# Attention's inverse sums as a diagonal factor in the transposes, in a two-layer sparse-attention and mixture trunk

## The chip, the cores and the metric

One NeuronCore of a Trainium2 chip runs the whole program. The metric is the device time of one execution in microseconds (us). The engines are TensorE (PE; its weight loads are PEld in the profile), VectorE (DVE), ScalarE (ACT), GpSimd (POOL) and SyncE (SP, which issues the weight DMAs). Each takes its own instructions in order; semaphores tie them together.

## The reference

Two layers, each of a mixer and a mixture of experts over 512 tokens of width 1024. The change concerns the attention of the mixer only. Its core, cut:

```python
score = einsum(relu(q_idx . k_idx), w_idx)            # indexer, 8 heads
_, sel = lax.top_k(where(admissible, score, -inf), 128)
logits = einsum('bqhd,bqkhd->bqhk', qb, k_sel) * att_scale   # 8 heads of 64
p = softmax(where(sel_ok, logits, -inf), axis=-1)
y_a = einsum('bqhk,bqkhd->bqhd', p, v_sel)            # queries in 4 blocks of 128
...
x = x + concat([y_a, y_pool, y_conv]) @ w_out
x = x + hier_moe(rmsnorm(x))                          # 16 experts, 6 MB of weights each
```

The softmax divides by the sum of the exponentials. The kernel does not gather: it adds a mask to the full row of logits, so that keys not chosen come out as zero.

## The kernel before, in words

Each layer projects the input (products of float32 split into a high and a low half, three products each), runs the indexer and 16 rounds of top-k on VectorE while TensorE makes the later projections, then the attention stage, the output projection, routing, and 16 experts whose weights stream through a ring of slots.

The attention stage is 16 **units**: query block b = unit // 4 (128 queries, 128·(b+1) keys) and head pair j = unit % 4, with d = 0, 1 the two heads of the pair. The order is written out by hand as a software pipeline over **steps** s:

- TensorE in step s: the logits of unit s (`unit_qk`, L1015), the transposes of unit s−2 (`unit_turn`, L1039, one `T.transpose` of 128x128 for each head and key block), the product with V of unit s−3 (`unit_pv`, L1029), in steps 7, 11, 15 and 17 the spreading of inverse sums (`spread_rinv`, L1049), in steps 10 and 11 the convolution branch's products (L1089), in 12 and 13 the pooling branch's (L1099). Units 0 to 2's logits and unit 0's transposes are interleaved with the projection of V. Before the logits of steps 4, 5 and 6 stand 4, 2 and 2 products of constants (`spin`, L693) that nobody reads.
- VectorE in step s: mask and row minimum of unit s (L1983, two instructions; its output is the buffer `probs[s % 2]`, so it waits until unit s−2 has been transposed), then `other(s)`: low halves of output weights in steps 4, 7, 10 and 15 (`lo`, L436), the branches' low halves in steps 11 to 14 (L1961, L1966), in steps 5, 9, 13 reciprocals of 8 sums (`o_inverse`, L1943), in 8, 12, 16 `o_scale` (L1951 copies the spread inverses out of bank 2, L1952 multiplies PV's bank with them into `osb`), and one step later `o_lo` (L1935). After `other`, in steps 3 to 9, one part of the pooling branch (L1619 to L1636).
- ScalarE: exponentials of unit s with their sums into `stat` (`unit_exp`, L1377), copies of the transposed unit s−2 to SBUF (`unit_pt`, L1385), and in its own `other` the high halves (L431, L1365, L1393, L1398).

The logits of both heads have one bank each, so `unit_qk(s)` waits until VectorE has read both of unit s−1. After the last step TensorE goes straight on to the output projection. A matmul whose operands are float32 is two records in the trace; a transpose, and a product of the split halves, is one.

Of the kernel before, what the change touches and what calls it, by code (L numbers as in the profile page):

```python
# [111 lines left out]
SPREAD_UNIT, SCALE_UNIT, HALF_UNIT = (7, 11, 15, 17), (8, 12, 16), (9, 13, 17)  # L112
# [39 lines left out]
def trunk(nc, t, out):  # L152
    with ExitStack() as ctx:
# [72 lines left out]
        osb = ar(A_O, 512)  # L226
# [38 lines left out]
        for name, dims in (("lg", (TT, 20)), ("gd", (TT, 4)), ("ge", (TT, 4)), ("og", (TT, 4)), ("key", (E - FIXED,)), ("place", (E,)), ("perm", (E,)),   # L265
# [49 lines left out]
        qk_ready, logit_set, exp_set, pt_ready, pt_set, pv_ready, rinv_set, r_ready, o_set = (  # L315
            sem(n) for n in ("qk_ready", "logit_set", "exp_set", "pt_ready", "pt_set", "pv_ready", "rinv_set", "r_ready", "o_set"))
# [370 lines left out]
        def _(pe):  # L687
# [290 lines left out]
            for l in range(DEPTH):  # L978
# [39 lines left out]
                def unit_pv(w):  # L1018

                    b, j = w // PAIRS, w % PAIRS  # L1020
                    if w == 0:
                        pe.wait_ge(v_set, 4 * (l + 1))
                    pe.wait_ge(pt_set, HEAD_UNITS * l + 2 * w + 2)
                    if j == 0 and b >= 2:
                        pe.wait_ge(o_set, TT * l + b - 1)
                    for kb in range(b + 1):
                        for d in range(2):
                            h = 2 * j + d
                            mm = T.matmul(ps[d * 64:d * 64 + 64, b % 2, j * P:(j + 1) * P], v_sb[:, kb, h * HD:(h + 1) * HD],  # L1029
                                          pTs[w % 2][:, d, kb * P:(kb + 1) * P], start=(kb == 0), stop=(kb == b))  # L1030
                    mm.then_inc(pv_ready, 1)

                def unit_turn(w):
                    for d in range(2):
                        pe.wait_ge(exp_set, HEAD_UNITS * l + 2 * w + d + 1)
                        if w:
                            pe.wait_ge(pt_set, HEAD_UNITS * l + 2 * w - 1 + d)
                        for kb in range(w // PAIRS + 1):
                            mm = T.transpose(ps[:, 6 + d, kb * P:(kb + 1) * P], probs[w % 2][:, d, kb * P:(kb + 1) * P], ident)  # L1039
                        mm.then_inc(pt_ready, 1)  # L1040

                def spread_rinv(b):

                    pe.wait_ge(rinv_set, TT * l + b + 1)
                    if b:
                        pe.wait_ge(o_set, TT * l + b)
                    for j in range(PAIRS):
                        for d in range(2):
                            mm = T.matmul(ps[d * 64:d * 64 + 64, 2, j * P:(j + 1) * P],  # L1049
                                          rinv[:, 2 * j + d:2 * j + d + 1].to_broadcast([P, HD]), ident, start=True, stop=True)  # L1050
                    mm.then_inc(r_ready, 1)
# [64 lines left out]
                for s in range(len(QK_AT), UNITS + 3):  # L1116
# [8 lines left out]
                    if s in SPREAD_UNIT:  # L1125
                        spread_rinv(SPREAD_UNIT.index(s))
# [10 lines left out]
                for i in range(4):  # L1137
                    use(pe, n + i)
                    for tt in ((2, 3, 1, 0) if i == 0 else range(TT)):
                        if i == 0 and tt == 1:  # L1140
                            pe.wait_ge(o_set, TT * (l + 1))
                        for h in range(2):
                            mm = out_product(i, tt, h)
                    mm.then_inc(w_used, 1)
# [45 lines left out]
        def _(sc):  # L1190
# [103 lines left out]
            for l in range(DEPTH):  # L1294
# [68 lines left out]
                def o_hi(b):  # L1363
                    sc.wait_ge(o_set, TT * l + b + 1)
                    A.activation(a_hi[:, 0:4, b * P:(b + 1) * P], osb.rearrange("p (q n) -> p q n", q=4),  # L1365
# [96 lines left out]
        def _(ve):  # L1462
# [402 lines left out]
            for l in range(DEPTH):  # L1865
# [67 lines left out]
                def o_lo(b):  # L1933
                    ve.wait_ge(o_hi_set, TT * l + b + 1)
                    V.tensor_tensor(a_lo[:, 0:4, b * P:(b + 1) * P], osb.rearrange("p (q n) -> p q n", q=4),  # L1935
                                    a_hi[:, 0:4, b * P:(b + 1) * P].bitcast(F32), ALU.subtract).then_inc(o_lo_set, 1)

                def o_inverse(b):

                    ve.wait_ge(exp_set, HEAD_UNITS * l + HEADS * (b + 1))  # L1940
                    if b:
                        ve.wait_ge(r_ready, TT * l + b)
                    V.reciprocal(rinv[:], stat[:, 1, HEADS * b:HEADS * (b + 1)]).then_inc(rinv_set, 1)  # L1943

                def o_scale(b):

                    ve.wait_ge(r_ready, TT * l + b + 1)
                    ve.wait_ge(pv_ready, UNITS * l + PAIRS * (b + 1))
                    if b:
                        ve.wait_ge(o_lo_set, TT * l + b)  # L1950
                    link(V.tensor_copy(osb, ps[:, 2, :]))  # L1951
                    V.tensor_tensor(osb, ps[:, b % 2, :], osb, ALU.mult).then_inc(o_set, 1)  # L1952

                def other(s):
# [13 lines left out]
                    if s in (5, 9, 13):  # L1968
                        o_inverse((s - 5) // PAIRS)
                    if s - 1 in HALF_UNIT:  # L1970
                        o_lo(HALF_UNIT.index(s - 1))
                    if s in SCALE_UNIT:
                        o_scale(SCALE_UNIT.index(s))

                def unit(s):
# [9 lines left out]
                    other(s)  # L1985
                    if 3 <= s < 10:
                        pooling(l, s - 3)
# [33 lines left out]
                for s in range(4, UNITS):  # L2021
                    unit(s)
                other(UNITS)
                o_inverse(TT - 1)
                other(UNITS + 1)
                other(UNITS + 2)
                o_scale(TT - 1)
# [112 lines left out]
```

## Time and profile before

| | |
|---|---|
| median of 3 runs | 1111.81 us (1110.94 to 1113.27) |
| the profiled execution | 1111.22 us, of which the profile's span is 1108.9 us |
| TensorE busy | 1043.9 us (94%) |
| VectorE, ScalarE busy | 548.9 us (49%), 292.3 us (26%) |
| granted TensorE clock, mean | 0.984 |

The span is cut by what TensorE does: projections and indexer from 0 to 151 us, attention (steps 3 to 18, from the logits of unit 3 to the output projection) from 165.7 to 221.0 us, output projection and routing to 285 us, experts to 520 us, then the second layer with the same stages 545.94 us later. A time in a row is counted from the start of the span. A row's duration holds its latency, and records of one engine overlap: how fast instructions follow each other is read from the distance of starts.

### The profile page before, as it was taken

What the parts mean: (1) busy time and instruction counts of PE and PEld (TensorE: products, weight loads), DVE (VectorE), ACT (ScalarE), POOL (GpSimd) and SP (SyncE); (2) the same over time, 40 slices, a digit from 0 to 9 for tenths busy, and PEclk for the clock granted to TensorE, in tenths of its full rate; (3) what the DMA queues carried; (4) which work ended last, traced back from release to release, by engine and by line L of the source; (5) the groups of instructions that cost most, each with busy time, mean ns of one, the idle gap of its engine ahead of it and who ended that gap; (6) DMA issues with size and microseconds to landing.
All of it is one profiled execution on the core that took longest, in us unless ns stands there. A gap on an engine that the chain in (4) does not pass through costs nothing.

```text
span 1108.9 us, 26835 instructions
## 1 busy us (share of the span) xinstructions
PE 1043.9 (94%) x11416; PEld 769.3 (69%) x11416; DVE 548.9 (49%) x1260; ACT 292.3 (26%) x570; POOL 192.0 (17%) x265
## 2 busy tenths in 40 slices
PE   8999998999999999997889999989999999999875
PEld 7876874587778777763478677646877988677432
DVE  5999987525611111110679999764364012101108
ACT  5225346623000010010252343465230000000003
POOL 3300000000323332231300000000003332233220
PEclk9999999999999999998999999999999999999988
DMA  9742211054989999999944122012479799999994
GB/s 358 235 193 77 84 50 57 21 209 179 405 319 341 401 401 403 406 403 406 351 147 133 57 89 92 24 45 70 177 289 396 269 394 404 402 402 404 407 399 188
DMA packets 86903, 279.63 MB, mean 252 GB/s; under 512 B 12344, under 2 KB 12448, under 8 KB 86768
## 3 DMA queue, kind: packets, MB, share of 16 engines
q1 hardware_dynamic: 71040, 237.60, 56.3%
q0 software_dynamic: 15728, 40.15, 10.0%
q8 instruction: 94, 1.54, 0.6%
q14 instruction: 41, 0.34, 0.1%
HBM read 257.43 MB, written 23.07 MB: 253 GB/s over the span
## 4 chain that ended last, share of the span: by engine, by line
PE 69%; DVE 15%; DMA 6%; issue 3%; ACT 3%; SPq 3%; POOL 1%; POOLq 0%; DVEq 0%; ACTq 0%
PE ps L852 24%; PE ps L892 11%; DVE arena L1611 7%; PE ps L455 7%; PE ps L457 7%; PE ps L456 7%; DMA arena<-in_w_dn 3%; SPq L406 3%; DVE w_lo L436 2%; PE ps L1039 2%; PE ps L1015 1%; PE ps L1029 1%; PE ps L998 1%; DMA arena<-y_rows,yidx 1%; PE ps L693 1%
## 5 line engine op out<-in xcount | busy, mean ns | idle before, releaser
L1827 DVE SCALAR_TENSOR_TENSOR arena<-ps,gslot,arena 128x128 f32<-128x128 f32 x88 | 25.7, 345 | 385.6 <-ACT arena L1250 368.4
L852 PE MATMUL ps<-arena 128*32 128x256 f32 x2624 | 155.3, 380 | 3.8 <-DMA arena<-in_w_gu 2.8
L852 PE MATMUL ps<-raw,arena 128*32 128x256 f32 x2528 | 149.9, 380 | 6.9 <-DMA raw<-in_w_gu 6.2
L852 PEld LDWEIGHTS ps<-arena 128*32 128x32 f32 x2624 | 113.0, 110 | 41.6 <-issue 8.0
L852 PEld LDWEIGHTS ps<-raw,arena 128*32 128x32 f32 x2528 | 102.8, 110 | 48.7 <-DMA raw<-in_w_gu 12.4
L631 POOL DMA_INDIRECT gain<-h_rows,tab x82 | 85.0, 1036 | 249.1 <-DVE arena L1819 206.1
L455 PE MATMUL ps<-a_hi,w_hi 128*128 128x512 f32 (+1 forms) x304 | 121.7, 400 | 3.1 <-DVE w_lo L436 2.1
L457 PE MATMUL ps<-a_hi,w_lo 128*128 128x512 f32 (+1 forms) x304 | 118.7, 390 | 0.0
L456 PE MATMUL ps<-a_lo,w_hi 128*128 128x512 f32 (+1 forms) x304 | 118.6, 390 | 0.0
L431 ACT ACTIVATE w_hi<-raw 128x1024 fp32r<-128x1024 f32 (+1 forms) x64 | 65.0, 1022 | 131.9 <-PE ps L457 130.7
L1250 ACT ACTIVATE arena<-ps 128x384 f32<-128x384 f32 (+1 forms) x32 | 14.9, 465 | 308.8 <-PE ps L852 266.9
L436 DVE TENSOR_TENSOR w_lo<-raw,w_hi 128x1024 fp32r<-128x1024 f32 (+1 forms) x64 | 74.8, 1172 | 34.5 <-ACT w_hi L431 34.3
L1611 DVE SCALAR_TENSOR_TENSOR arena<-arena,chan 128x512 f32<-128x512 f32 x120 | 84.2, 747 | 1.3
L640 POOL DMA_DIRECT2D y_rows<-arena x112 | 63.2, 575 | 101.9 <-ACT arena L1258 97.6
L892 PE MATMUL ps<-arena,pw 128*32 128x256 f32 x1088 | 68.3, 399 | 8.4 <-DMA arena<-in_w_dn 8.4
L455 PE MATMUL ps<-w_hi,a_hi 128*128 128x512 f32 x192 | 76.2, 397 | 0.0
L457 PE MATMUL ps<-w_hi,a_lo 128*128 128x512 f32 x192 | 74.9, 390 | 0.0
L456 PE MATMUL ps<-w_lo,a_hi 128*128 128x512 f32 x192 | 74.8, 390 | 0.0
L455 PEld LDWEIGHTS ps<-a_hi,w_hi 128*128 128x128 f32 (+1 forms) x304 | 56.3, 185 | 22.6 <-issue 7.7
L892 PE MATMUL ps<-raw,arena 128*32 128x256 f32 x1184 | 71.0, 379 | 0.6 <-DMA raw<-in_w_dn 0.6
L577 POOL DMA_DIRECT2D gain<-in_norm_g x2 | 1.1, 540 | 398.5 <-PE ps L1029 398.5
L457 PEld LDWEIGHTS ps<-a_hi,w_lo 128*128 128x128 f32 (+1 forms) x304 | 56.3, 185 | 13.2
(260 smaller groups left out, 1437.8 us busy)
## 6 DMA issues: line engine op xcount, KB each, us to landing
arena<-in_w_gu SPq DMA_DIRECT2D x120, 512.0 KB
raw<-in_w_gu SPq DMA_DIRECT2D x116, 512.0 KB
raw<-in_w_dn SPq DMA_DIRECT2D x68, 512.0 KB
arena<-in_w_dn SPq DMA_DIRECT2D x48, 512.0 KB
raw<-in_w_in SPq DMA_DIRECT2D x40, 512.0 KB
deep<-in_w_gu SPq DMA_DIRECT2D x20, 512.0 KB, 7.6
y_rows<-arena POOLq DMA_DIRECT2D x96, 96.0 KB
raw<-in_w_out SPq DMA_DIRECT2D x16, 512.0 KB
```

The costliest lines, as they stand in the source:

```text
L406: sp.dma_start(at_slot(slot_of[n], w), src.rearrange("p (a n) -> p a n", a=2)).then_inc(landed(n)[0], 16)
L431: nc.scalar.activation(split_slot(w_hi, k, w), at_slot(slot_of[n], w), ACT.Copy).then_inc(w_hi_set, 1)
L436: nc.vector.tensor_tensor(split_slot(w_lo, k, w), at_slot(slot_of[n], w), split_slot(w_hi, k, w).bitcast(F32), ALU.subtract).then_inc(w_lo ...
L455: nc.tensor.matmul(o, lh, rh, start=start, stop=False)
L456: nc.tensor.matmul(o, lh, rl, start=False, stop=False)
L457: return nc.tensor.matmul(o, ll, rh, start=False, stop=stop)
L631: pool.indirect_dma_start(xg[:, s * QC:(s + 1) * QC], None, h2q[l], bass.IndirectOffsetOnAxis(ap=tab[:, s, e:e + 1], axis=0), bounds_check ...
L640: pool.dma_start(rows[c], ysb[G * c:G * c + G, 0:GROUPS_OF[e] * QC].rearrange("i (s n) -> i s n", n=QC)).then_inc(y_stored, 16)
L852: mm = T.matmul(o, rows, piece[:, :, c * P:(c + 1) * P], start=b == 0, stop=b == 7)
L892: mm = T.matmul(ps[G * c:G * c + G, D_BANK + s, 0:QC], act, piece[:, c // 2, c % 2 * QC:(c % 2 + 1) * QC], start=b == 0, stop=b == 3)
L1611: V.scalar_tensor_tensor(out=acc[:, m, :], in0=src, scalar=w, in1=acc[:, m, :], op0=ALU.mult, op1=ALU.add).then_inc(conv_tap, 1)
L1827: ins = V.scalar_tensor_tensor(out=slu[:, s, :], in0=hidden(e, 1)[:, s, :], scalar=gslot[:, s, e:e + 1], in1=slu[:, s, :], op0=ALU.mult, o ...
```

## The change

`spread_rinv`, `o_inverse`, `o_scale` and the buffer `osb` go. For each unit, VectorE now takes the reciprocals of its two sums and multiplies the identity with each, which makes two 128x128 diagonals in the place of `osb` (two units deep). The transpose of the probabilities becomes an ordinary float32 product of the probabilities with that diagonal, which transposes and scales at once. The high and low halves of the output are then taken directly from PV's bank, and the waits on `o_set` become waits on `o_lo_set`, `pv_ready` and `diag_set`.

```diff
-SPREAD_UNIT, SCALE_UNIT, HALF_UNIT = (7, 11, 15, 17), (8, 12, 16), (9, 13, 17)
+HALF_UNIT = (7, 11, 15)
...
-        osb = ar(A_O, 512)
+        diags = ar(A_O, 512).rearrange("p (u d n) -> p u d n", u=2, d=2)
...
                     if j == 0 and b >= 2:
-                        pe.wait_ge(o_set, TT * l + b - 1)
+                        pe.wait_ge(o_lo_set, TT * l + b - 1)
...
                 def unit_turn(w):
                     for d in range(2):
-                        pe.wait_ge(exp_set, HEAD_UNITS * l + 2 * w + d + 1)
+                        pe.wait_ge(diag_set, UNITS * l + w + 1)
                         if w:
                             pe.wait_ge(pt_set, HEAD_UNITS * l + 2 * w - 1 + d)
                         for kb in range(w // PAIRS + 1):
-                            mm = T.transpose(ps[:, 6 + d, kb * P:(kb + 1) * P], probs[w % 2][:, d, kb * P:(kb + 1) * P], ident)
+                            mm = T.matmul(ps[:, 6 + d, kb * P:(kb + 1) * P], probs[w % 2][:, d, kb * P:(kb + 1) * P], diags[:, w % 2, d, :],
+                                          start=True, stop=True)
                         mm.then_inc(pt_ready, 1)
-                def spread_rinv(b):
...
-                    if s in SPREAD_UNIT:
-                        spread_rinv(SPREAD_UNIT.index(s))
...
-                        if i == 0 and tt == 1:
-                            pe.wait_ge(o_set, TT * (l + 1))
+                        if i == 0 and tt == 0:
+                            pe.wait_ge(o_lo_set, TT * (l + 1))
...
                 def o_hi(b):
-                    sc.wait_ge(o_set, TT * l + b + 1)
-                    A.activation(a_hi[:, 0:4, b * P:(b + 1) * P], osb.rearrange("p (q n) -> p q n", q=4),
+                    sc.wait_ge(pv_ready, UNITS * l + PAIRS * (b + 1))
+                    A.activation(a_hi[:, 0:4, b * P:(b + 1) * P], ps[:, b % 2, :].rearrange("p (q n) -> p q n", q=4),
                                  ACT.Copy).then_inc(o_hi_set, 1)
...
-                def o_inverse(b):
...
-                def o_scale(b):
...
+                def unit_diag(w):
+
+                    q = 2 * w
+                    inverse = rinv[:, q % HEADS:q % HEADS + 2]
+                    ve.wait_ge(exp_set, HEAD_UNITS * l + q + 2)
+                    V.reciprocal(inverse, stat[:, 1, q:q + 2]).then_inc(rinv_set, 1)
+                    ve.wait_ge(rinv_set, UNITS * l + w + 1)
+                    V.tensor_tensor(diags[:, w % 2], ident.unsqueeze(1).to_broadcast([P, 2, P]), inverse.unsqueeze(2).to_broadcast([P, 2, P]),
+                                    ALU.mult).then_inc(diag_set, 1)
...
                     other(s)
+                    if s:
+                        unit_diag(s - 1)
                     if 3 <= s < 10:
                         pooling(l, s - 3)
...
+                unit_diag(UNITS - 1)
                 other(UNITS)
-                o_inverse(TT - 1)
                 other(UNITS + 1)
                 other(UNITS + 2)
-                o_scale(TT - 1)
                 o_lo(TT - 1)
```

In VectorE's order, steps 7 and 8 of the first layer before (the last mask instruction of step 7 on; L436 is the low half, L1632 the pooling branch, L1951 and L1952 `o_scale`):

```order
L1983 ISA arena,stat<-ps,arena 128x256
L1983 ISA stat 128x1
L436 TENSOR_TENSOR w_lo<-raw,w_hi 128x1024
L1632 SCALAR_TENSOR_TENSOR arena<-arena,cst 64x512 x2
L1983 ISA arena,stat<-ps,arena 128x384
L1983 ISA stat 128x1
L1983 ISA arena,stat<-ps,arena 128x384
L1983 ISA stat 128x1
L1951 COPY arena<-ps 128x512
L1952 TENSOR_TENSOR arena<-ps,arena 128x512
L1632 SCALAR_TENSOR_TENSOR arena<-arena,cst 64x512 x2
```

The same place now (in the changed file L1961 is the mask instruction, L1931 and L1933 the diagonals, L1620 the pooling branch, L1923 `o_lo`):

```order
L436 TENSOR_TENSOR w_lo<-raw,w_hi 128x1024
L1931 RECIPROCAL rinv<-stat 128x2
L1933 TENSOR_TENSOR arena<-cst,rinv 128x256
L1620 SCALAR_TENSOR_TENSOR arena<-arena,cst 64x512 x2
L1961 ISA arena,stat<-ps,arena 128x384
L1961 ISA stat 128x1
L1961 ISA arena,stat<-ps,arena 128x384
L1961 ISA stat 128x1
L1923 TENSOR_TENSOR a_lo<-ps,a_hi 128x4x128
L1931 RECIPROCAL rinv<-stat 128x2
L1933 TENSOR_TENSOR arena<-cst,rinv 128x256
L1620 SCALAR_TENSOR_TENSOR arena<-arena,cst 64x512 x2
```

Copy and multiply have gone from step 8, where the low half of the output now stands, and a reciprocal and a product with the identity stand in every step, behind `other` and ahead of the pooling branch.

VectorE's last steps of the first layer before (step 15 on):

```order
L1983 ISA arena,stat<-ps,arena 128x512
L1983 ISA stat 128x1
L436 TENSOR_TENSOR w_lo<-raw,w_hi 128x1024
L1951 COPY arena<-ps 128x512
L1952 TENSOR_TENSOR arena<-ps,arena 128x512
L1943 RECIPROCAL rinv<-stat 128x8
L1935 TENSOR_TENSOR a_lo<-arena,a_hi 128x4x128
L1951 COPY arena<-ps 128x512
L1952 TENSOR_TENSOR arena<-ps,arena 128x512
L1935 TENSOR_TENSOR a_lo<-arena,a_hi 128x4x128
L436 TENSOR_TENSOR w_lo<-raw,w_hi 128x1024 x4
```

And now (from the second head's mask of step 15):

```order
L1961 ISA arena,stat<-ps,arena 128x512
L1961 ISA stat 128x1
L436 TENSOR_TENSOR w_lo<-raw,w_hi 128x1024
L1931 RECIPROCAL rinv<-stat 128x2
L1933 TENSOR_TENSOR arena<-cst,rinv 128x256
L1931 RECIPROCAL rinv<-stat 128x2
L1933 TENSOR_TENSOR arena<-cst,rinv 128x256
L1923 TENSOR_TENSOR a_lo<-ps,a_hi 128x4x128 x2
L436 TENSOR_TENSOR w_lo<-raw,w_hi 128x1024 x4
```

The diagonals of units 14 and 15 stand behind the low half of step 15 (L436).

TensorE from step 15 to the end of the stage, before (L1015 logits, L1039 transposes, L1029 product with V, L1049 the spreading):

```order
L1015 MATMUL ps<-arena 128x512 x2
L1039 MATMUL ps<-cst,arena 128x128 x8
L1029 MATMUL ps<-arena 64x128 x8
L1049 MATMUL ps<-cst,rinv 64x128 x8
L1039 MATMUL ps<-cst,arena 128x128 x8
L1029 MATMUL ps<-gain,arena 64x128 x8
L1039 MATMUL ps<-cst,arena 128x128 x8
L1029 MATMUL ps<-arena 64x128 x8
L1049 MATMUL ps<-cst,rinv 64x128 x8
L1029 MATMUL ps<-gain,arena 64x128 x8
```

And now (L1039 is the product with the diagonal):

```order
L1015 MATMUL ps<-arena 128x512 x2
L1039 MATMUL ps<-arena 128x128 x8
L1029 MATMUL ps<-arena 64x128 x8
L1039 MATMUL ps<-arena 128x128 x8
L1029 MATMUL ps<-gain,arena 64x128 x8
L1039 MATMUL ps<-arena 128x128 x8
L1029 MATMUL ps<-arena 64x128 x8
```

Each spreading row is gone and each transpose has become a float32 product.

## Rows read from the trace of the kernel before

**Rows 1.** The page's fourth part: chain that ended last, share by engine.

```profile
PE 69%; DVE 15%; DMA 6%; issue 3%; ACT 3%; SPq 3%; POOL 1%; POOLq 0%; DVEq 0%; ACTq 0%
```

**Rows 2.** Groups of TensorE instructions by form: xcount, busy us, mean ns, idle before.

```profile
L1039 PE MATMUL ps<-cst,arena 128*128 128x128 f32 x160 | 28.3, 296 | 4.7 <-ACT arena L1385 4.3
L1049 PE MATMUL ps<-cst,rinv 128*64 128x128 f32 x128 | 8.3, 273 | 0.0
L714 PE MATMUL ps<-arena,x_sb 128*128 128x128 f32 x32 | 3.9, 275 | 0.0
```

**Rows 3.** Timeline of TensorE, 8.8 to 15 us: start, duration, instructions.

```profile
10.28 2.78 PE L713 MATMUL ps<-cst,arena 128*128 128x128 f32 x24
12.90 1.95 PE L714 MATMUL ps<-arena,x_sb 128*128 128x128 f32 x16
```

**Rows 4.** Timeline of TensorE in the first layer's attention.

```profile
171.34 0.70 PE L1015 MATMUL ps<-arena 64*128 64x256 f32 x4
...
174.39 0.70 PE L1015 MATMUL ps<-arena 64*128 64x256 f32 x4 [0.59 <-DVE stat L1983]
...
179.84 0.92 PE L1015 MATMUL ps<-arena 64*128 64x384 f32 x4
...
186.54 1.28 PE L1015 MATMUL ps<-arena 64*128 64x384 f32 x4 [1.35 <-DVE stat L1983]
187.75 1.54 PE L1039 MATMUL ps<-cst,arena 128*128 128x128 f32 x6
...
192.22 0.92 PE L1015 MATMUL ps<-arena 64*128 64x384 f32 x4
193.07 0.87 PE L1039 MATMUL ps<-cst,arena 128*128 128x128 f32 x6
...
194.58 1.04 PE L1049 MATMUL ps<-cst,rinv 128*64 128x128 f32 x16
195.55 1.98 PE L1089 MATMUL ps<-arena,pw 128*128 128x512 f32 x4
197.47 1.13 PE L1015 MATMUL ps<-arena 64*128 64x512 f32 x4
...
202.30 1.13 PE L1015 MATMUL ps<-arena 64*128 64x512 f32 x4
...
207.14 1.13 PE L1015 MATMUL ps<-arena 64*128 64x512 f32 x4
208.20 1.09 PE L1039 MATMUL ps<-cst,arena 128*128 128x128 f32 x8
...
210.37 1.13 PE L1015 MATMUL ps<-arena 64*128 64x512 f32 x4 [0.27 <-DVE stat L1983]
...
214.81 1.40 PE L1039 MATMUL ps<-cst,arena 128*128 128x128 f32 x8
...
220.96 0.50 PE L455 MATMUL ps<-w_hi,a_hi 128*128 128x512 f32 x1
```

**Rows 5.** Timeline of VectorE in the same stretch.

```profile
178.95 1.22 DVE L436 TENSOR_TENSOR w_lo<-raw,w_hi 128x1024 fp32r<-128x1024 f32 x1
180.08 1.50 DVE L1632 SCALAR_TENSOR_TENSOR arena<-arena,cst 64x512 f32<-64x512 f32 x2
...
182.58 0.69 DVE L1951 COPY arena<-ps 128x512 f32<-128x512 f32 x1
183.30 0.69 DVE L1952 TENSOR_TENSOR arena<-ps,arena 128x512 f32<-128x512 f32 x1
...
205.95 0.19 DVE L1943 RECIPROCAL rinv<-stat 128x8 f32<-128x8 f32 x1
```

**Rows 6.** Line L1902, a product with a broadcast operand.

```profile
L1902 DVE TENSOR_TENSOR rw<-rw,gcol x1: 476/476/476, 44.0 to 44.0; 128x320 f32<-128x320 f32 x1
```

**Rows 7.** Windows: width, busy of PE, PEld, DVE, ACT, POOL; clock; DMA share; GB/s.

```profile
187.00:190.00 3.00, 3.00 (x18) 1.86 (x14) 1.12 (x5) 2.00 (x7) 0.00 (x0) 0.50 0.00 0
...
310.00:330.00 20.00, 20.00 (x373) 16.83 (x366) 4.85 (x14) 1.78 (x3) 6.37 (x8) 1.00 0.87 329
```

## What the change will do to the time, and why

> **What bounds the kernel now.** I read the chain of waits first [rows 1]: TensorE holds 69% of it, VectorE 15%, DMA 6%. So a microsecond of TensorE work counts unless it falls into a gap. Next come the forms of the instructions that change [rows 2], then how fast such instructions follow each other [rows 3], because durations of overlapping records say little. The timelines of the attention stage [rows 4, 5] show a pipeline that is nearly closed. TensorE's time between starts of a step's logits is 5.25 us in step 11 (192.22 to 197.47), 4.83 us in step 12 (to 202.30), 3.23 us in step 14 (207.14 to 210.37), and only gaps of 0.3 to 1.4 us stand in it, all until VectorE has masked the logits. One more thing is to be seen: in step 10 (186.54 to 192.22, 5.68 us) the logits take 1.28 us where step 11's take 0.92 us, since the granted clock from 187 to 190 us was 0.50, the 1.2 GHz level, after TensorE had sat idle for 1.35 us [rows 4, 7].
>
> **The products.** `T.transpose` is one record: 160 in two layers, 80 a layer [rows 2]. A float32 product is two. L714 is such a product with a diagonal, as the new ones are, and shows its pace: L713's 24 transposes start at 10.28 and L714 at 12.90 us, 2.62/24 = 0.109 us each; L714's 16 records, for 8 products, take 1.95 us with a tail of some 0.16 us, 0.112 us each [rows 3]. So a product costs two times a transpose, and 80 more records a layer are 80 x 0.11 = 8.8 us. The spreading goes: 64 records a layer, 0.97 us for the 16 of each block (194.58 to 195.55) [rows 2, 4], 3.9 us a layer. Net TensorE work +4.9 us a layer.
> The Trainium skill speaks against this edit: "Perfetto Trace Analysis", Transposes, asks that logical transposes use the transpose and not a standard matmul. Its page "TensorE: Matmul & The Clock Gate" (Terms) puts the transpose mode at 4 times the speed for float32; by that a product would add 0.33 us instead of 0.11 us, an estimate of 26 us a layer. The records of rows 3 say two times, and I take them.
>
> **The diagonals.** VectorE gets, for each of 16 units, a reciprocal of 128x2 and a product of 128x256. The reciprocal of 128x8 takes 0.19 us [rows 5]. A product with a broadcast operand of 128x320 takes 0.476 us [rows 6], so 128x256 takes some 0.42 us; the wait between the two costs little, as L1952 starts 0.72 us after L1951, whose duration is 0.69 us [rows 5]. Since starts follow closer than durations, I take 0.57 us a unit; bounds are 0.45 (full overlap) and 0.9 us (if broadcasting both operands were twice as slow). That is 9 us of VectorE a layer, against 4 x (0.19 + 1.4) = 6.4 us removed. It costs time only where TensorE waits for it: `unit_diag(s-1)` is behind the masks and `other` of step s, and TensorE's products of step s+1 need it. They stand behind the logits of step s+1, which give 0.42 to 1.06 us of cover. A low half (1.13 us, 178.95 to 180.08 [rows 5]) in `other` breaks that cover; it stands in steps 4, 7, 10, 15. Taking the halves from PV's bank costs nothing new: `o_hi` and `o_lo` leave a chain with the copy and multiply ahead of them, and the last `o_lo` must be done only after 18 products of the output projection, some 4 us. With it done some 1.5 us after the last PV, nothing waits.
>
> **Step by step, each layer**, with starts of the first layer [rows 4] (the second repeats them):
> - Up to step 10's start (186.54): the small turns of units 0 to 2 add 2 records each, 0.22 us, of which some 0.55 us in sum reaches step 5 (171.34). Diagonal 3 comes behind the low half of step 4, so TensorE, which had other waits of 0.3 us there, waits till some 2 us after step 5's start and step 6 starts 0.9 us late (174.39 before). Step 7's larger turn makes that 1.1 us; then the spreading goes and step 8 (179.84) is 0.3 us late. Diagonal 6 is behind the low half of step 7 and then the pooling branch's 1.50 us delays the masks; the 1.4 us of copy and multiply of step 8 go, 0.7 us of `o_lo` and 0.57 us of diagonal come. Step 10 starts 1.5 us late. **+1.5**
> - Step 10: logits 0.85, turn 0.80 + 0.65 for 6 more records, PV 0.5, the convolution product 1.92 us, 4.75 us in sum at full clock, where 5.68 us were. I take the low clock to go (below). **-0.9**
> - Step 11: no spreading, but L1089 must wait until VectorE has written the low half of the product before it, behind masks that follow the larger turn: 5.7 against 5.25 us. **+0.45**
> - Steps 12, 13: the pooling product waits in the same way; the second mask starts after both turns instead of back to back with the first, 0.43 us later each. **+0.85**
> - Step 14: turn 1.05 -> 1.88 us (8 more records), and the next logits wait for the second mask: 3.23 -> 3.97 us. **+0.75**
> - Step 15 to the turn of unit 14 (210.37 to 214.81, 4.44 us): TensorE would need 1.2 + 1.88 + 1.0 = 4.1 us, but diagonal 14 stands behind two masks that end 4.0 us after the step's start, the low half (1.13 us) and its own 0.57 us: 5.8 us, of which TensorE idles 1.7 us. **+1.35**
> - From there to the output projection (214.81 to 220.96): two turns with 8 more records each, +1.75 us, less the spreading (0.9) and a wait of 0.3 us. **+0.55**
>
> Sum 4.55 us a layer, 9.1 us in two. Behind the stage nothing takes it back: from 310 to 330 us the DMA share was 0.87, so the weights waited for slots there, and slots are freed by expert products that start after attention [rows 7]. The profiled execution's 1111.22 us + 9.1 = 1120.3 us; its own time is 0.6 us under the median of 1111.81, so the forecast is 1120.9, said as 1121 us, slower by 0.8%.
>
> **The rivals.**
> - *The low clock stays.* What speaks for it: TensorE still idles between steps 8 and 10 (some 3 us of 8). Against it: its busy share there is no smaller, with twice the records in the turns. Price: step 10 is then 1.5 us longer in each layer, +3.0 us: 1124 us. The page on the clock gate (PE-mode transpose) says that a transpose does not count as busy as a product does; by that the change itself would lift the clock. The trace shows only that the clock fell where transposes, gaps and small products mixed [rows 4, 7]; that bears on my choice a little.
> - *The diagonals come in time.* If ScalarE's and VectorE's orders slide so that waits at steps 5, 8 and 9 are hidden in waits that exist anyway, some 1.7 us a layer goes: 1117.5 us.
> - *Faster.* The masking and exponentials, not TensorE, set the period, and a second record runs in time that TensorE spends waiting. Then only the losses by diagonals stay: +0.9 up to step 10, -1.5 in step 10 (clock and nothing added), 0 in 11 to 14, +0.45 in step 15, -1.2 after it with the spreading gone: -1.35 us a layer, 1109 us. It decides if the gaps in steps 11 to 15 exceed 0.11 us x the added records (0.65 to 0.9 us). Rows 4 show gaps of 0.3 us in step 14 and 15, and none before the turns: against it.
> - *Slower still.* The idle 1.7 us ahead of unit 14's turn brings the clock down for the last turns, PV and the first output products (as after 186.54, 1.6 us for one fall), on top of the low clock at step 10: 1111.8 + 9.1 + 3.0 + 3.2 = 1127 us.
> - *Absorbed.* The experts end on weight transfers, and a longer attention lets the ring fill further: within 0.2%. Against it: the share of 0.87 above, and that the slots depend on attention's own end.
>
> **How the numbers follow.** Chances: forecast 0.47, low clock stays 0.20, diagonals in time 0.12, slower still 0.08, absorbed 0.06, faster 0.07. The range from 1114 to 1127 us takes in the first four and the ends of the cost of a diagonal (0.12 us less or 0.33 us more at some 5 places in each layer, -1.2 or +3.3 us). Within 0.2% (2.2 us, about what a measurement tells from no change) is 0.07, faster 0.07, slower 0.86.
>
> **What would show it.** In the new profile: two records for each product of the turns, at a pace of 0.11 us, 320 in all; none of L1049; the reciprocal and product of a unit in some 0.57 us; the granted clock near step 10; a gap of some 1.7 us ahead of unit 14's turn with VectorE's diagonal as its releaser; the stage (from the logits of unit 3 to the output projection) 59.8 us long where it was 55.2 us. The forecast is wrong if that stage grows by under 2 us, or if the experts start late and end in time.

## The result, and the profile after

The changed kernel takes 1124.55 us (median of 4 runs, 1123.56 to 1125.22) where the kernel before, measured with it, takes 1111.38 us (4 runs, 1108.71 to 1113.27). The ratio is 1.012, 95% interval 1.0097 to 1.0142: slower by 13.2 us, where the forecast was 9.1 us more and 1121 us. The profiled execution took 1123.56 us, span 1121.3 us, 12.4 us over the span before.

First the page of the kernel after: its busy row and the shares of the chain that ended last.

```profile
PE 1053.0 (94%) x11448; PEld 789.6 (70%) x11448; DVE 553.6 (49%) x1300; ACT 292.5 (26%) x570; POOL 192.0 (17%) x265
...
PE 68%; DVE 16%; DMA 6%; SPq 5%; issue 3%; ACT 2%; POOL 1%; DVEq 0%; POOLq 0%; ACTq 0%
```

TensorE is busy 9.1 us longer (1043.9 before), VectorE 4.7 us, and nothing has changed in who bounds the kernel [rows 1]. The groups by form show the edit itself (busy us, mean ns, idle before):

```profile
L1039 PE MATMUL ps<-arena 128*128 128x128 f32 x320 | 44.8, 286 | 8.8 <-DVE arena L1933 6.7 <-ACT arena L1373 1.8
...
L1933 DVE TENSOR_TENSOR arena<-cst,rinv 128x256 f32<-128x256 f32 x32 | 13.6, 425 | 1.1
```

L1039 has 320 records where it had 160, L1049 is gone [rows 2], and what ended most of TensorE's idle time before L1039 is now VectorE's diagonal (6.7 us), where it was ScalarE's copy (4.3 us). Busy time alone does not tell the price: the timeline does. Of TensorE in the first layer's attention, with step 3 at the top and the output projection's first product at the end:

```profile
165.61 0.49 PE L1015 MATMUL ps<-arena 64*128 64x128 f32 x4
...
171.67 0.70 PE L1015 MATMUL ps<-arena 64*128 64x256 f32 x4
...
173.19 0.71 PE L1039 MATMUL ps<-arena 128*128 128x128 f32 x4 [0.81 <-DVE arena L1933]
...
181.87 1.16 PE L1039 MATMUL ps<-arena 128*128 128x128 f32 x8 [0.76 <-DVE arena L1933]
...
188.00 0.92 PE L1015 MATMUL ps<-arena 64*128 64x384 f32 x4 [0.75 <-DVE stat L1961]
188.85 1.60 PE L1039 MATMUL ps<-arena 128*128 128x128 f32 x12
...
192.88 0.92 PE L1015 MATMUL ps<-arena 64*128 64x384 f32 x4
...
196.76 1.98 PE L1079 MATMUL ps<-arena,pw 128*128 128x512 f32 x4 [0.62 <-DVE a_lo L1943]
198.68 1.13 PE L1015 MATMUL ps<-arena 64*128 64x512 f32 x4
...
202.91 1.12 PE L1089 MATMUL ps<-arena,pbd 128*128 128x512 f32 x2 [0.76 <-DVE a_lo L1943]
...
209.25 1.13 PE L1015 MATMUL ps<-arena 64*128 64x512 f32 x4
210.30 2.05 PE L1039 MATMUL ps<-arena 128*128 128x128 f32 x16
212.29 0.88 PE L1029 MATMUL ps<-gain,arena 128*64 128x128 f32 x12
213.26 1.13 PE L1015 MATMUL ps<-arena 64*128 64x512 f32 x4
...
219.08 2.05 PE L1039 MATMUL ps<-arena 128*128 128x128 f32 x16 [1.55 <-DVE arena L1933]
...
225.96 0.50 PE L455 MATMUL ps<-w_hi,a_hi 128*128 128x512 f32 x1
```

Set against [rows 4], the stage from 165.61 to 225.96 takes 60.35 us, where it took 55.24 us (165.72 to 220.96). The second layer has 60.36 and 55.24 us. A turn with eight transposes (1.09 us) is a turn with 16 records (2.05 us). The 1.55 us wait stands where the prediction put it. VectorE in front of it:

```profile
216.65 0.69 DVE L1961 CUSTOM_DVE_ANT_0 arena<-ps,arena 128x512 f32<-128x512 f32 x1 [0.19 <-PE ps L1039]
...
217.27 1.22 DVE L436 TENSOR_TENSOR w_lo<-raw,w_hi 128x1024 fp32r<-128x1024 f32 x1
218.40 0.16 DVE L1931 RECIPROCAL rinv<-stat 128x2 f32<-128x2 f32 x1
218.60 0.43 DVE L1933 TENSOR_TENSOR arena<-cst,rinv 128x256 f32<-128x256 f32 x1
218.94 0.16 DVE L1931 RECIPROCAL rinv<-stat 128x2 f32<-128x2 f32 x1
```

The mask of step 15, the low half of an output weight, then the diagonal of unit 14, which is what TensorE waits for from 217.53 to 219.08 us. From reciprocal to reciprocal a diagonal takes 0.54 us. The clock in two windows (width, busy of the five engines, clock, DMA share, GB/s):

```profile
187.00:190.00 3.00, 2.25 (x20) 1.46 (x16) 1.62 (x8) 1.83 (x6) 0.00 (x0) 1.00 0.00 0
...
217.00:220.00 3.00, 1.45 (x18) 1.21 (x15) 2.93 (x8) 2.46 (x7) 0.00 (x0) 1.00 0.15 16
```

The first window had 0.50 before [rows 7]; now TensorE keeps 2.4 GHz there, and across the 1.55 us wait too.

Outside the attention stages a difference of 2.2 us is left. One microsecond of it lies between the layers. TensorE's products of constants there, after and then before:

```profile
557.47 0.79 PE L693 MATMUL ps<-cst 128*128 128x128 f32 x2 [3.76 <-DVE x_sb L1548]
...
561.45 0.79 PE L693 MATMUL ps<-cst 128*128 128x128 f32 x2 [3.19 <-issue]
```

```profile
552.02 3.67 PE L693 MATMUL ps<-cst 128*128 128x128 f32 x16 [3.67 <-DVE x_sb L1560]
```

"issue" is idle time that ended on nothing the profile shows: TensorE stood for 3.19 us in the middle of its products of constants. Before, the 16 products ran without a break. From the landing of the gathered rows of layer 1 to the first projection product of layer 2 (L455) it takes 16.39 us where it took 15.35. The rest is 0.4 us in the first layer's experts (271.5 against 271.1 us from their first product, L832, to that landing) and 0.6 us from the second layer's first expert product to the end (286.27 against 285.69).

### The profile page after: what moved, and what is told of

Its sections match the earlier page's. It is cut to its first block, busy times and chain, and to the rows that moved or that the text cites. A ratio compares the mean times of both kernels' runs of the same rounds, so it can differ in the third digit from the quotient of the medians.

```text
span 1121.3 us, 26919 instructions
## 1 busy us (share of the span) xinstructions
PE 1053.0 (94%) x11448; PEld 789.6 (70%) x11448; DVE 553.6 (49%) x1300; ACT 292.5 (26%) x570; POOL 192.0 (17%) x265
## 4 chain that ended last, share of the span: by engine, by line
PE 68%; DVE 16%; DMA 6%; SPq 5%; issue 3%; ACT 2%; POOL 1%; DVEq 0%; POOLq 0%; ACTq 0%
PE ps L852 23%; PE ps L892 10%; DVE arena L1599 7%; PE ps L455 7%; PE ps L457 7%; PE ps L456 7%; SPq L406 4%; DMA arena<-in_w_gu 3%; PE ps L1039 3%; DVE w_lo L436 2%; DVE arena L1961 1%; DMA arena<-in_w_dn 1%; PE ps L1015 1%; PE ps L693 1%; PE ps L897 1%
## 5 line engine op out<-in xcount | busy, mean ns | idle before, releaser
L852 PEld LDWEIGHTS ps<-arena 128*32 128x32 f32 x2624 | 115.4, 110 | 38.9 <-issue 8.4
L455 PE MATMUL ps<-a_hi,w_hi 128*128 128x512 f32 (+1 forms) x304 | 121.7, 400 | 2.8 <-DVE w_lo L436 2.1
L436 DVE TENSOR_TENSOR w_lo<-raw,w_hi 128x1024 fp32r<-128x1024 f32 (+1 forms) x64 | 74.7, 1169 | 37.6 <-ACT w_hi L431 37.4
L455 PE MATMUL ps<-w_hi,a_hi 128*128 128x512 f32 x192 | 76.1, 396 | 0.0
L455 PEld LDWEIGHTS ps<-a_hi,w_hi 128*128 128x128 f32 (+1 forms) x304 | 56.3, 185 | 22.3 <-issue 7.5
L892 PEld LDWEIGHTS ps<-arena,pw 128*32 128x32 f32 x1088 | 48.2, 116 | 26.1 <-issue 14.5
```

Of the source, the lines that this page charges most:

```text
L436: nc.vector.tensor_tensor(split_slot(w_lo, k, w), at_slot(slot_of[n], w), split_slot(w_hi, k, w).bitcast(F32), ALU.subtract).then_inc(w_lo ...
L455: nc.tensor.matmul(o, lh, rh, start=start, stop=False)
L852: mm = T.matmul(o, rows, piece[:, :, c * P:(c + 1) * P], start=b == 0, stop=b == 7)
L892: mm = T.matmul(ps[G * c:G * c + G, D_BANK + s, 0:QC], act, piece[:, c // 2, c % 2 * QC:(c % 2 + 1) * QC], start=b == 0, stop=b == 3)
```

## The experiments

The runs were made on four numbered chips: 4 (product alone, diagonals kept, transposes twice, diagonal first), 15 (kernel before again, late spins, scaling on VectorE), 11 (kernel after again, one product less, no division, spreading moved) and 5 (kernel before once more); the first measurement has no number. The kernel before has a median of 1103.07 to 1103.74 us on chips 4, 15 and 11, and takes 1111 to 1114 us in the first measurement and on chip 5. Where an expectation says "this chip" of a profile of before, it is one of the faster three. Each run is compared with runs of the kernel before from its own chip. "Stage" is always the distance from step 3's logits to the output projection's first product, read from a timeline, for the two layers. Where two theories stood in an expectation, it says which is A.

**One part alone: the product in place of the transpose.** The kernel before, with no diagonal; only the record's kind changes.

```diff
-  mm = T.transpose(ps[:, 6 + d, ...], probs[w % 2][:, d, ...], ident)
+  mm = T.matmul(ps[:, 6 + d, ...], probs[w % 2][:, d, ...], ident, start=True, stop=True)
```

> The kernel before with one edit: each transpose of the probabilities is a float32 product with the identity; spreading, copy and multiply stay, and nothing waits for a diagonal. Theory A (second records are on the path): the stage from the logits of unit 3 to the output projection grows from 55.2 to about 60.5 us a layer (8.8 us of records, part in gaps, the low clock near step 10 gone), the whole to 1122 us (+10.7). Theory B (what costs is the wait for the diagonals; the second records run in gaps): stage within 1 us of 55.2, the whole within 2 us of before.

Measured: 1114.39 against 1103.74 us, ratio 1.0089 (1.0068 to 1.0111). The stages take 59.65 us each. The stage comes out as theory A had it (60.5 us) and not as theory B: this line alone brings most of what the whole change costs.

**One part undone: transposes again, diagonals kept.** The diagonals are made and waited for, but not used.

```diff
-  mm = T.matmul(ps[:, 6 + d, ...], probs[w % 2][:, d, ...], diags[:, w % 2, d, :], start=True, stop=True)
+  mm = T.transpose(ps[:, 6 + d, ...], probs[w % 2][:, d, ...], ident)
```

> The changed kernel with one edit: the turns are transposes with the identity again, one record each, but still wait for their diagonals, so the output isn't divided by the sums. Theory A: the stage falls from 60.3 to 54.5 us if the clock holds, or 56 us if it falls near step 10 again; the whole 1112 to 1115 us. Theory B: the stage stays within 1 us of 60.3 and the whole at 1124 us.

Its whole time (2255.64 us) says nothing: the undivided output changes the routing, and the kernel's path for overfull experts runs. The first layer's attention comes ahead of that. Its first and last row:

```profile
168.11 0.49 PE L1015 MATMUL ps<-arena 64*128 64x128 f32 x4
...
222.55 0.50 PE L455 MATMUL ps<-w_hi,a_hi 128*128 128x512 f32 x1
```

54.44 us, against 60.35 with products: 5.91 us a layer come from the products in the turns, as theory A had it (54.5 us).

**Is it the second record, or the kind?** The kernel before, with each transpose issued twice.

```diff
-  mm = T.transpose(ps[:, 6 + d, ...], probs[w % 2][:, d, ...], ident)
+  for _ in range(2):
+      mm = T.transpose(ps[:, 6 + d, ...], probs[w % 2][:, d, ...], ident)
```

> The kernel before with each transpose issued twice, so that TensorE is as busy in the turns as with products, but with transposes only. Theory C1 (the clock near step 10 follows how long TensorE is busy, whatever the instruction): granted clock 1.00 around step 10 in both layers, stage and time as in the run with products alone (1122 us). Theory C2 (transposes do not count for the clock): the clock is 0.50 there for some 3 us in both layers, and the time is 2 to 3 us above the run with products alone (1125 us).

Measured: 1113.04 us, ratio 1.0079 (1.0058 to 1.0101), stages 58.80 us each. A late turn, and the clock in step 10 of both layers, which starts at 189.51 and 735.68 us here:

```profile
222.34 1.97 PE L1040 MATMUL ps<-cst,arena 128*128 128x128 f32 x16
```

```profile
189.50:192.50 3.00, 2.99 (x25) 2.10 (x25) 1.16 (x5) 2.40 (x8) 0.00 (x0) 1.00 0.00 0
735.70:738.70 3.00, 3.00 (x25) 2.12 (x26) 1.16 (x7) 2.40 (x9) 0.00 (x0) 1.00 0.01 3
```

16 transposes in 1.97 us, 16 product records in 2.05: the count of records is the price (+4.81 us a layer on 53.99), with 0.85 us a layer left for the kind. The clock was 1.00 through both stages with only transposes in the turns, as theory C1 had it and not C2. The Trainium skill ("TensorE: Matmul & The Clock Gate", PE-mode transpose) says that a transpose does not count as busy in the same way; these two stages do not bear that out for this place. They are one execution, though, and the next run but one shows that the clock can also hold here with single transposes, so that the kind of instruction plays no part is likely and not shown.

**The order on VectorE.** The kernel after, with the diagonal ahead of the masks.

```diff
+  if s:
+      unit_diag(s - 1)      # ahead of the masks of step s
...
-  if s:
-      unit_diag(s - 1)      # was behind other(s)
```

> The changed kernel with the diagonal of unit s-1 made ahead of the masks of step s instead of behind them and other(s). Theory A: the wait of 1.55 us before unit 14's turn goes, and the waits before turns 3, 6 and 7 (0.8, 0.8, 0.2 us) go but return as later masks, since VectorE is full there; the stage 58.7 us, the whole 1121 us (3 us less than the changed kernel). Theory B (the diagonals' waits are the whole loss): the stage 55.5 us and the whole 1114 us.

Measured: 1114.49 us, ratio 1.0104 (1.0075 to 1.0134), stages 59.30 us each. The wait for the diagonal before unit 14's turn is gone; what stands there now is ScalarE's copy:

```profile
218.55 2.32 PE L1039 MATMUL ps<-arena 128*128 128x128 f32 x16 [0.40 <-ACT gain L1373]
```

1.05 us a layer come back, of the 1.65 us that theory A expected (58.7 us); theory B (55.5 us) falls. From step 3 to step 10 nothing does (22.37 us, was 22.39): no turn waits for a diagonal there any more, but the logits wait longer for their masks (1.58 us ahead of step 9, where it was 0.75). No kernel after was run on this chip to set the whole time against.

**The kernel before again, for the clock.** No edit.

> The kernel before, unchanged, for a profile from the chip of the following runs. Both theories: stage 55.2 us, clock 0.50 near step 10 in both layers; within 0.3% of the other runs of before.

It took 1101.61 us, its stages 55.25 and 53.99 us; the expected low clock in both layers was missed. The same place in the two layers, 0.49 us after the start of step 10 (186.51 and 727.97 us):

```profile
187.00:190.00 3.00, 3.00 (x18) 1.87 (x14) 1.12 (x5) 1.98 (x6) 0.00 (x0) 0.50 0.03 5
728.46:731.46 3.00, 2.92 (x21) 1.54 (x18) 1.92 (x5) 2.72 (x8) 0.00 (x0) 1.00 0.01 3
```

The same instructions, once at 1.2 GHz and once at 2.4: the fall comes in one layer and not in the other of one execution, and costs 1.25 us where it comes. What decides it no run shows.

**Spins against the low clock.** The kernel before with eight more products of constants.

```diff
+FILL_LATE = {9: 3, 10: 5}
...
+                    if s in FILL_LATE:
+                        spin(3, FILL_LATE[s])
```

> The kernel before with 3 unread products of constants ahead of the logits of step 9 and 5 ahead of those of step 10, into bank 3 (free there), where TensorE waits for masks anyway. Theory C1 (the clock falls near step 10 for want of TensorE work): clock 1.00 there in both layers, stage 53.7 us, the whole 3 us less than before. Rival (the clock falls once per stage wherever the gaps then are, or the extra products push the logits back): stage 55.2 us or more, the whole equal within 1 us.

Measured: 1103.74 (12 runs) against 1103.54 us (18 runs), ratio 1.0004 (0.9989 to 1.0018). Both stages take 53.99 us, clock 1.00, as theory C1 had it, but the whole time gains nothing. The 3 us were counted as if every stage of the kernel before had the low clock. Nor is it shown that the added products held it: the run before this one has a stage of 53.99 us without them. The profiled execution also lost 1.68 us elsewhere, to a low clock at the first products of the first layer's experts (below).

**Scaling on VectorE, with transposes.** The kernel after; the diagonals go, the probabilities are multiplied in place ahead of the masks of the next unit, each head as it comes, and the turns are transposes with the identity.

```diff
...
-  V.tensor_tensor(diags[:, w % 2], ident..., inverse..., ALU.mult).then_inc(diag_set, 1)
+  for d in range(2):
+      V.tensor_scalar(probs[w % 2][:, d, 0:K], probs[w % 2][:, d, 0:K], inverse[:, d:d + 1], None, ALU.mult).then_inc(diag_set, 1)
```

> The changed kernel with the probabilities themselves multiplied by the inverse sums on VectorE, in place, one instruction for each head, ahead of the masks of the next unit; the turns are transposes with the identity again, and spreading, copy and multiply stay gone. Theory A (the second records are the loss, the removal of the spreading a gain): stage 53.5 us, the whole 3 to 4 us less than before. Theory B (having to finish VectorE's work on a unit before its turn is the loss): stage 58 us or more, the whole 5 us above before.

Measured: 1107.78 us, ratio 1.0047 (1.0028 to 1.0066), stages 57.30 us (clock 0.54 from 190 to 193 us) and 55.93 us (0.62 and 0.50 in 722 to 725 and 725 to 728 us): between the theories, a miss for A. The clock fell in both stages, at different steps, so what the stage takes at the full clock is not known. The waits of TensorE in the whole execution point at the rest:

```profile
PE ps L1015 <- DVE stat L1963: 9.8, 10, 2.0
...
PE ps L1039 <- ACT gain L1372: 3.0, 4, 0.9
```

Logits wait 9.8 us for masks, in the kernel before 6.5: the multiplications (0.88 us for two heads at 512 keys) stand ahead of them. That they are the cause is read from the order and the waits, not tested.

**The kernel after again.** No edit.

> The changed kernel, unchanged, against the kernel before on one chip with more runs. Its two stages explain 2 x 5.1 = 10.2 us and an instruction wait of TensorE between the layers 1.0 us more. Theory N (the rest of the 13.2 us measured first is scatter): the difference is 11 us, within 1.5. Theory L (any edit costs some 2 us outside the stages): 13 us.

Measured: 1118.16 us (4 runs, 1117.68 to 1118.62) against 1103.07 (23 runs), ratio 1.0133 (1.0116 to 1.0151), +15.1 us. Both theories missed. The stages repeat (60.36 us twice), and the issue wait is 1.9 us and costs 0.2. The first layer's experts take 269.1 us to the landing of the rows, where the kernel before (on chip 15) and the kernel with one product less (below, on this chip) took 266.6; the last part, from the second layer's first expert product to the end, takes 283.95 us, against 282.0 and 281.3. Most of this is the clock. The experts' first products here in both layers, and under them the same products in the run with one product less:

```profile
282.71 7.07 PE L832 MATMUL ps<-arena 128*32 128x256 f32 x96 [0.15 <-DVE arena L1667]
...
832.25 7.07 PE L832 MATMUL ps<-arena 128*32 128x256 f32 x96 [0.15 <-DVE arena L1667]
```

```profile
277.61 5.39 PE L832 MATMUL ps<-arena 128*32 128x256 f32 x96 [0.15 <-DVE arena L1679]
```

The windows in the first of them, here and in the first profile of the kernel after:

```profile
282.00:285.00 3.00, 2.85 (x29) 1.62 (x32) 2.69 (x11) 1.31 (x2) 0.00 (x0) 0.63 0.96 378
```

```profile
282.00:285.00 3.00, 2.85 (x54) 1.70 (x56) 2.69 (x11) 0.88 (x1) 0.00 (x0) 1.00 1.03 415
```

1.68 us in each layer for the same 96 records, at a low clock that the first profile of the kernel after did not have. So the change does not bring it by itself; the late spins' profile, without the change, has it too. What is left, 0.8 us in the first stretch and 0.3 to 0.9 us in the last, is no more than these stretches differ by between the runs on chips 4, 15 and 11.

**Does any edit cost two microseconds?** The kernel before with one product of constants less in the first row of them.

```diff
-            spin(0, 28, zeros[:, 0:P], zeros[:, 0:P])
+            spin(0, 27, zeros[:, 0:P], zeros[:, 0:P])
```

> The kernel before with 27 instead of 28 unread products at the program's start, where TensorE waits for the input anyway: an edit that leaves the attention stage alone. Theory N: equal to before within 1 us. Theory L: 2 us slower.

Measured: 1103.13 against 1103.07 us, ratio 1.0003 (0.9991 to 1.0015): this edit does not. Its stages are 53.99 and 54.00 us. In the first layer, where the kernel before had 0.50:

```profile
187.00:190.00 3.00, 1.78 (x10) 0.92 (x10) 1.54 (x8) 2.36 (x7) 0.00 (x0) 1.00 0.00 0
```

**Neither diagonals nor spreading.** The kernel after with transposes that wait only for the exponentials, and no reciprocals or diagonals.

```diff
-  pe.wait_ge(diag_set, UNITS * l + w + 1)
+  pe.wait_ge(exp_set, HEAD_UNITS * l + 2 * w + d + 1)
...
-  unit_diag(s - 1)
```

> The changed kernel with plain transposes and without the reciprocals and diagonals, so nothing divides by the sums; only the first layer's stage can be read, since the routing behind it sees other numbers. With the clock held, theory A (removing spreading, copy and multiply is worth about what the waits for the diagonals take): stage 52.5 us, against 54.4 us with diagonals that are waited for and 54.0 us for the kernel before with the clock held. Theory S (the spreading lay in gaps and its removal is worth nothing): 54 us.

The first layer's attention, the whole time being of no use as in the run with the diagonals kept:

```profile
167.75 0.49 PE L1015 MATMUL ps<-arena 64*128 64x128 f32 x4
...
220.12 0.50 PE L455 MATMUL ps<-w_hi,a_hi 128*128 128x512 f32 x1
```

52.37 us, as theory A had it (52.5). With the run that keeps the diagonals and the stages above, a layer's stage at the full clock comes apart: 53.99 before; 52.37 without the division (−1.62: all that the edit could give back); 54.44 with the diagonals (+2.07); 60.35 with products (+5.91).

**A better place for the spreading.** The last run with spins, and the spreading of block 2 in the gap of step 13.

```diff
-SPREAD_UNIT, SCALE_UNIT, HALF_UNIT = (7, 11, 15, 17), (8, 12, 16), (9, 13, 17)
+SPREAD_UNIT, SCALE_UNIT, HALF_UNIT = (7, 11, 13, 17), (8, 12, 16), (9, 13, 17)
...
+  if s in (5, 9, 12): o_inverse(...)     # first in other(s)
```

> The kernel before with the late spins of the earlier run and the spreading of block 2 in step 13 instead of 15, where TensorE waits 1.04 us for VectorE ahead of the pooling product; its reciprocals come in step 12. Theory A: 0.9 us less a layer than with the spins alone, stage 53.1 us, the whole 3 us less than before. Rival: the spreading delays the pooling product or comes too late, stage 54 us, the whole equal to before.

Measured: 1104.12 against 1103.07 us, ratio 1.0006 (0.9994 to 1.0018), stages 54.05 us each. TensorE:

```profile
203.77 1.04 PE L1050 MATMUL ps<-cst,rinv 128*64 128x128 f32 x16
204.98 1.12 PE L1100 MATMUL ps<-arena,pbd 128*128 128x512 f32 x2 [0.17 <-DVE a_lo L1971]
...
213.28 0.63 PE L1040 MATMUL ps<-cst,arena 128*128 128x128 f32 x4 [0.39 <-ACT gain L1388]
...
214.47 0.63 PE L1040 MATMUL ps<-cst,arena 128*128 128x128 f32 x4 [0.56 <-ACT gain L1388]
...
552.29 3.58 PE L694 MATMUL ps<-cst 128*128 128x128 f32 x16 [8.11 <-issue]
```

The gap is filled, and what was moved out of step 15 comes back as two waits for ScalarE's copies: the rival was right. An issue wait of 8.11 us appears between the layers, of which 1.25 us cost time (16.60 us from the landing of the rows to the second layer's first product, against 15.35).

**The kernel before once more.** No edit.

> The kernel before, unchanged, for one more profile. If the low clock near step 10 is a matter of chance in each layer, its two stages are 55.2 or 54.0 us each, independently; if the stretch from the first expert product to the landing of the last gathered rows is 266.6 us in the kernel before on this chip (as in two profiles) and longer after an edit, it is within 0.3 us of 266.6; if that stretch merely scatters, it is anywhere from 266 to 271 us.

1112.28 us; stages 55.25 and 55.30; experts 271.61 us to the landing, where the first profile of before had 271.08 and the kernel after 271.5. This chip is as slow as the first measurement, so the run does not settle what was expected of 266.6 us; it shows the experts of the kernel before as long as those of the first kernel after. No version tried beats the kernel before.

## Why the prediction was right, and where its size was off

The direction, the bound and nearly all the waits came as forecast. By the prediction's own steps, for each layer, predicted and measured:

| | predicted | measured |
|---|---|---|
| up to step 10 | +1.5 | +1.57 |
| step 10 | −0.9 | −0.80 |
| step 11 | +0.45 | +0.55 |
| steps 12, 13 | +0.85 | +0.90 |
| step 14 | +0.75 | +0.78 |
| step 15 to unit 14's turn | +1.35 | +1.38 |
| rest | +0.55 | +0.73 |
| sum | +4.55 | +5.11 |

- *The products.* Two records for one: shown, by the count (320) and by issuing the transpose twice. That the pace would be 0.11 us was slightly low: 8.8 us were counted for 80 records a layer, and by the pace of the turns, below, they are 9.6. A turn of eight transposes is followed by PV after 1.03 us (208.20 to 209.23 us before), one of 16 records after 1.99 us (210.30 to 212.29): 0.96 us for eight more, 0.12 us each. This is the term of the sum that was mis-sized within the stage, and the step "rest" with its two large turns shows it most. The Trainium skill's factor of 4 ("TensorE: Matmul & The Clock Gate", Terms), from which an estimate made 26 us a layer, is not borne out: the stage grew by 5.66 us in the run with the product alone. Its rule in "Perfetto Trace Analysis" (Transposes), to use the transpose for a logical transpose, is borne out: that line alone is a ratio of 1.0089.
- *The diagonals.* 0.54 us for each, against 0.57; with both operands broadcast the product took 425 ns where 0.42 us was forecast. The price of the diagonals and of the waits for them is 2.07 us a layer, shown by two runs that differ in them alone.
- *The wait before unit 14's turn.* 1.7 us forecast, 1.55 found; taking it away in the run with the diagonal first gave 1.05 us of it back.
- *The clock.* It held at step 10, as chosen, and the rivals with a low clock fell. Part of this is luck, since I took the low clock for a fixture of the kernel before, and there it comes and goes. It was low in five of the six stages profiled of the unedited kernel and held in one, and with one product less at the start of the program it held in both. Where it came it cost 1.25 us, and the rival took 1.5. So the credit of 0.9 us at step 10 belongs to the profiled execution; against a kernel whose clock held, the stage grows by 6.36 us. That is 2.5 us more over two layers where both would have held; the low clock at the experts' first products is 3.4 us in the profiled execution of the kernel after again. I infer that the two make the difference on chip 11 (+15.1 us) larger; how often each comes in the runs without a profile is not known.
- *Rivals.* "Diagonals in time" fell by the 1.57 us up to step 10, with waits for diagonals of 0.81 and 0.76 us in steps 5 and 8; "faster" by the product alone; "absorbed" by the experts, which took 271.5 us to the landing after a stage 5.1 us longer, as in the kernel before (271.1 and 271.6); "slower still" by the clock of 1.00 across the 1.55 us wait.
- *A gap overlooked.* The prediction has every gap of the stage end with a mask, and none large in steps 11 to 15. Two of 1.04 us stood ahead of the pooling products of steps 12 and 13, and were larger than the time of the records added there, which is what would have decided for the rival "faster":

```profile
201.25 1.12 PE L1099 MATMUL ps<-arena,pbd 128*128 128x512 f32 x2 [1.04 <-DVE a_lo L1961]
```

They took up little: 0.76 us of each is still there after, because the low half that ends them came later too, as the step's own term of the sum had it.
- *The chances.* Those of the slower outcomes add up to 0.87 and "absorbed" has 0.06, where the closing sentence has 0.86 and 0.07. Nothing hangs on it.
- *What failed.* That nothing was counted but the attention stages. The 12.4 us of span are 2 x 5.1 in the stages, of which 1.1 us above forecast, 1.0 at TensorE's issue wait between the layers, which I had not foreseen, and 1.1 in two stretches of experts, which is within what unedited runs differ by (0.5 us, 271.08 to 271.61, in each).

Open: what makes the issue wait. It was 3.2 us in the kernel after and 3.3 us with the diagonal first, 1.9 us in the kernel after again, 8.1 us with the spreading moved, and cost nothing in six other kernels (15.3 us from the landing to the second layer in each); it was not tried by itself. Also open is what makes the clock fall in one execution or layer and hold in another, at step 10 as at the experts' first products.

## What to carry to other kernels

Before replacing a transpose by a product that does something else as well, count records: a float32 product is two where a transpose is one, and here the saved work (1.6 us a layer) was a quarter of what the second records cost (5.9 us) on the engine that bounds the stage. Work taken off a busy engine and put on the idler one is only free where nothing behind it is waited for: put such a producer ahead of unrelated work and look at what its consumer then waits for. When a stretch shows a low clock, take a second profile of the same kernel before crediting a gain to its removal, and look for the same fall elsewhere when two kernels differ by more than the stage that was changed.

## What the runs showed of the hardware that I had not expected

- The granted clock of one and the same stretch falls to 0.50 or stays at 1.00 from layer to layer (55.25 and 53.99 us in one execution).
- The experts' first products (96 records) take 7.07 us at the low clock and 5.39 us at the full one, in executions with the same order of work around them.
- With each transpose issued twice the granted clock was 1.00 through both stages of the one execution profiled.
- TensorE stood for 1.9 to 8.1 us on nothing that the profile shows between the layers, in kernels whose code differs only in the attention stage; at most 1.25 us of it cost time.
- A VectorE product with both operands broadcast, 128x256, takes 425 ns; one with a broadcast operand, 128x320, took 476 ns [rows 6].
